# A 100-pair top-16 search, doubled lookup indices, and 44 row products beside the building of the gate table

## The chip, the core and the metric

The kernel runs on one core of one Trainium2 chip. The metric is the device time of one execution in microseconds (us). A run of a kernel is judged by the median of its executions.

## The reference, cut to what matters

The program is one step of a two-layer network for 384 tokens: 128 prompt tokens and 256 sample tokens. Each layer mixes the tokens by attention and then passes them through a retrieval of experts, which is where the change lies:

```
s1 = einsum('thd,nd->thn', q[..., :half], sub_k1)      # 8 heads, 128 keys
s2 = einsum('thd,nd->thn', q[..., half:], sub_k2)
v1, i1 = top_k(s1, 16);  v2, i2 = top_k(s2, 16)
cand_s = v1[..., :, None] + v2[..., None, :]           # 16 x 16 pairs per token and head
cand_i = i1[..., :, None] * 128 + i2[..., None, :]
top_s, pos = top_k(cand_s, 16)
idx = take_along_axis(cand_i, pos);  g = softmax(top_s)
out = sum over the 8 x 16 picks:  g * gelu(u_tab[idx] . x) * v_tab[idx]
```

The tables u and v have 16384 rows of 1024 numbers. Each token picks 8 x 16 = 128 of them.

## The kernel before, in words

The five engines have programs of their own, written out by hand, and meet at semaphores. No scheduler moves anything: the order in the code is the order on each engine. Both layers have the same experts part, about 900 us in each layer.

**Two ways through the tables.** For the 256 sample tokens the kernel computes against *all* rows: the tables are streamed in as 128 blocks of 128 experts, each block one 512 KB u chunk and one 512 KB v chunk. `hidden(b)` multiplies a u chunk with the tokens, ScalarE applies gelu, VectorE multiplies with the block's part of a gate table G (zero where an expert was not picked), which is `product(b)`, and `outer(b)` multiplies the result with the v chunk. For the 128 prompt tokens the kernel fetches just the picked rows: for each of 128 picks GpSimd issues one indirect DMA, which brings one u row for every token (128 x 1024 numbers, 512 KB). `dot(k)` on VectorE makes the row product. Later 128 more such DMAs bring the v rows, and `accumulate(k)` adds them up.

**Stages of the experts part of a layer.**

1. *Hidden stage.* TensorE does `hidden(0)` to `hidden(PLAIN - 1)`, `PLAIN` = 36, while VectorE searches: `top16` (five VectorE instructions per list: MAX8, FIND_INDEX8, MATCH_REPLACE8, MAX8, FIND_INDEX8) over lists of 128 key scores, then `winners`, which adds the 16 x 16 pairs and takes the 16 best of 256, then `pairs`, which turns places into key numbers by comparing with an iota, multiplying with the key numbers and reducing. ScalarE takes the exponents of the scores after gelu 12 (prompt) and gelu 29 (sample). `picks` then turns the results round on TensorE.
2. *Table stage.* TensorE does the `hidden` blocks that are left up to 63, and between them the 32 pieces of G (8 tokens each, `build(p)`); `pieces_of` spreads the pieces evenly over the blocks from `PLAIN` to `BUILT` = 62. For each piece VectorE makes four one-hot tensors (`one_hots(p)`), and after some of them an early `dot`. The early rows have only two places in memory (slots 4 and 5), as the four others lie where the one-hots are: the gather of row r + 2 waits for dot r.
3. *Middle stage.* TensorE does the 64 outer products of blocks 0 to 63; their gelu results come back from DRAM. VectorE does a product and about one dot for each (`MIDDLE_DOTS` = 72 in all). Rows have six slots from here on.
4. *Late stage.* For blocks 64 to 127 TensorE alternates `hidden(b + 1)`, now in three exact parts with u split into a high half (ScalarE) and a low half (VectorE, `low_u`), and `outer(b)`. VectorE does for each block a product, a `low_u`, and three rows: first the dots that are left (128 - 15 - 72 = 41), then from block 80 on the 128 sums, spread over 44 blocks.

**Queues.** SyncE loads all chunks in order into a ring of four slots, each load waiting until the slot is used up. In the late stage the loads go v, u, v, u. GpSimd issues the gathers in order. VectorE works strictly in order: when a `dot` waits for its row, the one-hots or products behind it wait too, and with them TensorE.

The lines that the prediction speaks of: 966 `hidden` in stages 1 and 2, 945 `build`, 931 `picks`, 977 `outer`, 670 to 672 `hidden` in the late stage, 1733 to 1745 `top16`, 1787 to 1793 `pairs`, 1834 to 1839 the one-hots, 1848 `product`, 1859 `low_u`, 1868 `dot`, 1882 `accumulate`, 1236 the high half of u, 589 the gathers.

Of the kernel before, what the change touches and what calls it, by code (L numbers as in the profile page):

```python
# [22 lines left out]
U32 = mybir.dt.uint32  # L23
# [17 lines left out]
HEADS = 8  # L41
TOPK = 16
KEYS = 128
STOK = TOK - P
# [3 lines left out]
SPILL = 64  # L48
PLAIN = 36
BUILT = 62  # L50
ROWS = 6
FULL = 4
EARLY_DOTS = 15
MIDDLE_DOTS = 72
GLS = 4
# [66 lines left out]
Q_IT = Q_IOE + KEYS // 2  # L122
Q_SW = Q_IT + 2 * STOK
Q_RING = Q_G - ROWS * D
# [43 lines left out]
def build(nc, a):  # L168
    ctx = ExitStack()
    with ctx:  # L170
# [129 lines left out]
        IOT = ar(Q_IOT, OA_N).bitcast(F16).rearrange("p (e t) -> p e t", e=KEYS)  # L300
        IT16 = ar(Q_IT, 2 * STOK).bitcast(F16).rearrange("p (q t) -> p q t", q=4)
        MROW = ar(A_MROW, 1024).rearrange("p (i n) -> p i n", i=2)
# [749 lines left out]
        def _(act):  # L1052
# [128 lines left out]
            def experts(l):  # L1181
# [29 lines left out]
                for b in range(SPILL):  # L1211
                    gelu(b)
                    if b == 12:
                        exponents(0, 0, P)
                    if b == 29:
                        exponents(1, P, STOK)
                    if b == PLAIN - 1:
                        for q in range(3):
                            act.wait_ge(sem("pick_ps"), since("pick_ps", l) + q + 1)
                            fn(IT16[:, q, :] if q < 2 else SW, ps[:, 3 + q, 0:STOK], ACT.Copy,  # L1220
                               scale=1.0 if q < 2 else G_SCALE).then_inc(sem("it_ready"), 1)
                    if b >= PLAIN:
                        for p in pieces_of(b):
                            part(p)
# [17 lines left out]
                for b in range(SPILL, KEYS):  # L1242
                    if b == SPILL:
                        gelu(b)
                    if b + 2 < KEYS:
                        high_u(b + 2)
                    if b + 1 < KEYS:
                        gelu(b + 1)
                    if b == SPILL + 15:
# [133 lines left out]
        def _(dve):  # L1383
# [337 lines left out]
            def retrieve(l):  # L1721
# [3 lines left out]
                dve.tensor_copy(IOT, iota.unsqueeze(2).to_broadcast([P, KEYS, PIECE]))  # L1725
                dve.tensor_copy(IOE, iota)

                IF16 = ar(Q_IF, NT * 128).bitcast(F16)
# [23 lines left out]
                dve.tensor_copy(IF16, ar(Q_I, NT * 256).bitcast(U32))  # L1752

# [4 lines left out]
                Tf = ar(Q_TV, NT * 128).rearrange("p (m n) -> p m n", n=TOPK)  # L1758
                IFh = IF16.rearrange("p (t h j n) -> p t h j n", t=NT, h=HEADS, j=2)
                eq = ar(Q_EQ, 1024).bitcast(F16)  # L1760

                def winners(first, last):

                    for t in range(first, last):
                        ins = tt(ar(Q_S + 2048 * t, 2048).rearrange("p (h a b) -> p h a b", h=HEADS, a=TOPK),
                                 Vh[:, t, :, 0, :].unsqueeze(3).to_broadcast([P, HEADS, TOPK, TOPK]),
                                 Vh[:, t, :, 1, :].unsqueeze(2).to_broadcast([P, HEADS, TOPK, TOPK]), ALU.add)
                    link(ins)
                    top16([(C[:, t, h, :], TV[:, t, h, :], TP[:, t, h, :])
                           for t in range(first, last) for h in range(HEADS)])  # L1770
                    m = slice(HEADS * first, HEADS * last)
                    link(dve.tensor_copy(ss[:, m], Tf[:, m, 0]))
                    tt(Tf[:, m], Tf[:, m], ss[:, m].unsqueeze(2).to_broadcast([P, HEADS * (last - first), TOPK]),
                       ALU.subtract).then_inc(sem("tv_ready"), 1)

                def pairs(first, last):

                    r, n = P * first, P * (last - first)
                    pos = ar(Q_TP + r, n).bitcast(U32)
                    ts(ar(Q_AB + r, n).bitcast(U32), pos, 4, None, ALU.logical_shift_right)  # L1780
                    link(ts(ar(Q_AB + 384 + r, n).bitcast(U32), pos, 15, None, ALU.bitwise_and))
                    for j in range(2):
                        ins = dve.tensor_copy(ar(Q_ABF + 384 * j + r, n), ar(Q_AB + 384 * j + r, n).bitcast(U32))
                    link(ins)
                    for j in range(2):
                        for t in range(first, last):
                            link(tt(eq.rearrange("p (m n) -> p m n", n=TOPK),
                                    ar(Q_ABF + 384 * j + 128 * t, 128).unsqueeze(2).to_broadcast([P, 128, TOPK]),
                                    iota[:, 0:TOPK].unsqueeze(1).to_broadcast([P, 128, TOPK]), ALU.is_equal))
                            e4 = eq.rearrange("p (h k n) -> p h k n", h=HEADS, k=TOPK)  # L1790
                            link(tt(e4, e4, IFh[:, t, :, j, :].unsqueeze(2).to_broadcast([P, HEADS, TOPK, TOPK]),
                                    ALU.mult))
                            link(dve.tensor_reduce(ar(Q_ID + 128 * (NT * j + t), 128),
# [24 lines left out]
            def experts(l):  # L1818
                at = {name: since(name, l) for name in ("gelu", "w_ready", "g_ps", "e1_ready", "row_used")}

                dve.wait_ge(sem("it_ready"), since("it_ready", l) + 3)
                link(dve.tensor_copy(IT16[:, 2, :], SW))
                link(tt(IT16[:, 3, :], SW, IT16[:, 2, :], ALU.subtract))

                def one_hots(p):
# [12 lines left out]
                    tt(high, low, over(2), ALU.mult)  # L1838
                    tt(low, low, over(3), ALU.mult).then_inc(sem("oh_ready"), 1)

# [64 lines left out]
                for b in range(SPILL, KEYS):  # L1905
# [12 lines left out]
                    if b == SPILL + 16:  # L1918
# [130 lines left out]
```

## Time and profile before

| | |
|---|---|
| median of 3 executions | 2618.59 us (2615.31 to 2625.87) |
| the profiled execution | 2623.26 us, its span 2621.4 us |
| TensorE (PE) busy | 2436.7 us, 93% of the span |
| VectorE (DVE) busy | 1707.4 us, 65% |
| GpSimd (POOL) busy | 914.4 us, 35% |
| ScalarE (ACT) busy | 639.3 us, 24% |
| moved by DMA | 679.61 MB |

Busy shares are means over stages with different limits, so they say little here. The windows view gives the same per stage, the timeline lists single instructions with the idle time ahead of them, and the chain of waits is followed back from the last instruction.

### The profile page before, as it was taken

The page shows a single profiled execution, that of the slowest core. Times are in us where ns is not written, and L with a number is a line of the kernel's source. Part 1 is how long each engine was busy: PE and PEld are TensorE (multiplying, and loading weights), DVE is VectorE, ACT ScalarE, POOL GpSimd, SP SyncE. Part 2 cuts the span into 40 slices and gives each one's busy share as a digit, 9 for nine tenths or more (in the row PEclk, how much of TensorE's full clock was granted, in tenths as well). Part 3 has the DMA queues.
Part 4 walks back from the last instruction along what each step waited for, and adds up shares of the span by engine and source line. Part 5 has one row for each costly group of instructions (what it writes and reads, how often), then busy time and mean ns, then how long its engine had stood idle before and what let it go on. Part 6 is the DMA issues. An engine that isn't in the chain of part 4 may idle for free.

```text
span 2621.4 us, 32722 instructions
## 1 busy us (share of the span) xinstructions
PE 2436.7 (93%) x12294; PEld 1755.8 (67%) x12294; DVE 1707.4 (65%) x3380; ACT 639.3 (24%) x1190; POOL 914.4 (35%) x650
## 2 busy tenths in 40 slices
PE   5988889999999999999978778999999999999995
PEld 4756689889544566666656567988974446666663
DVE  1345479979544676777645446897965457678775
ACT  2354441123000122222243344212320002221221
POOL 3400360001333454566353214200123335456550
PEclk8999989999999999999989798999999999999997
DMA  6455334656899999999835612265679999999992
GB/s 261 138 178 192 131 112 128 206 184 210 326 353 363 349 402 354 384 397 399 309 114 154 190 35 87 98 207 180 208 262 366 366 359 369 356 380 384 398 389 93
DMA packets 219899, 679.61 MB, mean 259 GB/s; under 512 B 32384, under 2 KB 63152, under 8 KB 219232
## 3 DMA queue, kind: packets, MB, share of 16 engines
q1 hardware_dynamic: 142912, 396.42, 43.2%
q0 software_dynamic: 76832, 281.11, 28.4%
q8 instruction: 99, 1.62, 0.2%
q14 instruction: 56, 0.46, 0.1%
HBM read 658.87 MB, written 18.56 MB: 258 GB/s over the span
## 4 chain that ended last, share of the span: by engine, by line
PE 73%; DMA 10%; DVE 8%; issue 4%; ACT 4%; SPq 1%; POOL 1%; ACTq 0%; DVEq 0%
PE ps L977 26%; PE ps L966 17%; DMA ring<-in_u 8%; PE ps L670 6%; PE ps L671 6%; PE ps L672 6%; DVE arena L1882 3%; PE ps L945 2%; PE ps L852 2%; PE ps L833 2%; ACT u_split L1236 1%; PE ps L693 1%; PE ps L842 1%; PE ps L701 1%; PE ps L920 1%
## 5 line engine op out<-in xcount | busy, mean ns | idle before, releaser
L977 PE MATMUL ps<-ring,arena 128*128 128x512 f32 x2048 | 903.8, 594 | 25.4 <-DVE arena L1848 24.7
L977 PEld LDWEIGHTS ps<-ring,arena 128*128 128x128 f32 x2048 | 379.7, 190 | 464.9 <-issue 464.7
L589 POOL DMA_INDIRECT arena<-in_u_rows,arena x256 | 300.1, 1172 | 856.1 <-DVE arena L1868 663.8
L966 PE MATMUL ps<-arena,ring 128*128 128x256 f32 x2048 | 454.1, 380 | 0.0
L589 POOL DMA_INDIRECT arena<-in_v,arena x256 | 355.7, 1389 | 252.9 <-DVE arena L1882 170.8
L966 PEld LDWEIGHTS ps<-arena,ring 128*128 128x128 f32 x2048 | 385.1, 190 | 50.0
L549 POOL TENSOR_TENSOR ring_lo<-ring,ring_hi 128x1024 fp32r<-128x1024 f32 x84 | 216.5, 2588 | 435.8 <-ACT ring_hi L1077 435.7
L1882 DVE SCALAR_TENSOR_TENSOR arena<-arena 128x1024 f32<-128x1024 f32 x254 | 325.8, 1282 | 19.4 <-DMA arena<-in_v,arena 1.9
L670 PE MATMUL ps<-xs_split,u_split 128*128 128x256 f32 x1024 | 336.2, 328 | 0.7 <-DVE u_split L1859 0.6
L1868 DVE CUSTOM_DVE_ANT_0 arena<-arena 128x1024 f32<-128x1024 f32 x256 | 307.1, 1220 | 8.5 <-DMA arena<-in_u_rows,arena 8.5
L1236 ACT ACTIVATE u_split<-ring 128x1024 fp32r<-128x1024 f32 x128 | 135.5, 1058 | 700.5 <-DMA ring<-in_u 660.5
L671 PE MATMUL ps<-xs_split,u_split 128*128 128x256 f32 x1024 | 289.3, 282 | 0.0
L672 PE MATMUL ps<-xs_split,u_split 128*128 128x256 f32 x1024 | 289.2, 282 | 0.0
L1859 DVE TENSOR_TENSOR u_split<-ring,u_split 128x1024 fp32r<-128x1024 f32 x128 | 156.8, 1225 | 180.2 <-ACT u_split L1236 164.3
L1848 DVE SCALAR_TENSOR_TENSOR arena<-arena 128x256 f32<-128x256 f32 x256 | 108.0, 423 | 243.6 <-DMA arena<-gelu_half 214.5
L670 PEld LDWEIGHTS ps<-xs_split,u_split 128*128 128x128 f32 x1024 | 195.4, 191 | 36.2 <-issue 36.2
L671 PEld LDWEIGHTS ps<-xs_split,u_split 128*128 128x128 f32 x1024 | 195.8, 191 | 27.3 <-issue 27.0
L1195 ACT ACTIVATE arena<-ps 128x256 f32<-128x256 f32 x256 | 97.3, 380 | 436.6 <-PE ps L966 338.4
L672 PEld LDWEIGHTS ps<-xs_split,u_split 128*128 128x128 f32 x1024 | 195.5, 191 | 0.0
L670 PE MATMUL ps<-ring_hi,x_hi 128*128 128x512 f32 (+2 forms) x312 | 122.2, 392 | 10.6 <-POOL x_lo L567 8.4
L671 PE MATMUL ps<-ring_lo,x_hi 128*128 128x512 f32 (+2 forms) x312 | 120.4, 386 | 0.0
L672 PE MATMUL ps<-ring_hi,x_lo 128*128 128x512 f32 (+2 forms) x312 | 120.1, 385 | 0.0
(223 smaller groups left out, 2736.8 us busy)
## 6 DMA issues: line engine op xcount, KB each, us to landing
ring<-in_u SPq DMA_DIRECT2D x256, 512.0 KB
ring<-in_v SPq DMA_DIRECT2D x256, 512.0 KB
ring<-in_w_mod SPq DMA_DIRECT2D x80, 512.0 KB
ring<-in_w_in SPq DMA_DIRECT2D x36, 512.0 KB
ring<-in_w_q SPq DMA_DIRECT2D x32, 512.0 KB
gelu_half<-arena SPq DMA_DIRECT2D x120, 128.0 KB, 3.5
arena<-gelu_half SPq DMA_DIRECT2D x120, 128.0 KB
arena<-in_w_mod SPq DMA_DIRECT2D x16, 512.0 KB, 18.9
```

Source lines behind the costliest of these rows:

```text
L549: pool.tensor_tensor(slot_lo[pos], slot[pos], f32(slot_hi[pos]), ALU.subtract).then_inc(lo_done(pos), 1)
L589: pool.indirect_dma_start(row[at], None, table, bass.IndirectOffsetOnAxis(where[:, k:k + 1], axis=0)).then_inc(sem(f"row_in{at}"), 16)
L670: mm(out, x[0], y[0], start=first, stop=False, skip_group_check=check)
L671: mm(out, x[0], y[1], start=False, stop=False, skip_group_check=check)
L672: return mm(out, x[1], y[0], start=False, stop=last, skip_group_check=check)
L966: ins = mm(ps[:, 6 + b % 2, 0:STOK], slot[c % RING][:, P * k:P * k + P], HFS[:, k, :], start=(k == 0), stop=(k == KC - 1))
L977: ins = mm(ps[:, t + 3 * q, :], GL[:, b % GLS, P * t - P:P * t], slot[c % RING][:, 512 * q:512 * q + 512], start=(b == MIDDLE[0]), stop=(b ...
L1236: fn(u_half(b, 0), slot[u_chunk(l, b) % RING], ACT.Copy).then_inc(sem("us_hi"), 1)
L1848: stt(w, w, 1.0 / G_SCALE, G[:, b, :], ALU.mult, ALU.mult).then_inc(sem("w_ready"), 1)
L1859: tt(u_half(b, 1), slot[c % RING], f32(u_half(b, 0)), ALU.subtract).then_inc(used(c % RING), 1)
L1868: dve.tensor_tensor_reduce(row[row_slot[k]], row[row_slot[k]], HP, 1.0, 0.0, ALU.mult, ALU.add, HSEL[:, k:k + 1]).then_inc(sem("row_used"), 1)
L1882: stt(HP, x, WSEL[:, k:k + 1], HP, ALU.mult, ALU.add).then_inc(sem("row_used"), 1)
```

## The change

Three things are changed together, and five constants with them.

*The search.* Of the 256 pairs of two sorted lists only those can be among the best 16 whose places i and j (from 0) meet (i + 1)(j + 1) <= 16. The new lists hold the first three i with all 16 j, and the other 13 i with the first four j: 3 x 16 + 13 x 4 = 100 pairs. The place in the list no longer is 16 i + j, so `pairs` finds the first key by comparing the place with the 16 starts of the rows and adding up differences of key numbers, and the second by a few more small instructions.

*The doubled indices.* Numbers that were read once and spread over the last dimension are now stored twice side by side, in 16 bits, and spread so that the last dimension is a run of two: in the comparisons of `pairs` (32 bits before) and in the second one-hot of a piece (16 bits before).

*The row products.* `EARLY_DOTS` goes from 15 to 44 and may be two after one piece, `MIDDLE_DOTS` from 72 to 60, so that 24 dots (41 before) are left for the late stage. `PLAIN` goes from 36 to 27, so the table stage has 35 blocks in place of 26 for the same 32 pieces. The sums start at block 76 and are spread over 48 blocks. The exponents are taken after gelu 10 and 20.

```diff
+WIDE, THIN = 3, 4
+CANDS = WIDE * TOPK + (TOPK - WIDE) * THIN
-PLAIN = 36
+PLAIN = 27
-EARLY_DOTS = 15
-MIDDLE_DOTS = 72
+EARLY_DOTS = 44
+MIDDLE_DOTS = 60
+SUMS = SPILL + 4 + (KEYS - EARLY_DOTS - MIDDLE_DOTS) // 3
...
-                    if b == 12:
+                    if b == 10:
                         exponents(0, 0, P)
-                    if b == 29:
+                    if b == 20:
                         exponents(1, P, STOK)
...
+                            if q == 1:
+                                fn(PAIRED, ps[:, 4, 0:STOK].unsqueeze(2).to_broadcast([P, STOK, 2]), ACT.Copy
+                                   ).then_inc(sem("it_ready"), 1)
...
-                        ins = tt(ar(Q_S + 2048 * t, 2048).rearrange("p (h a b) -> p h a b", h=HEADS, a=TOPK),
-                                 Vh[:, t, :, 0, :].unsqueeze(3).to_broadcast([P, HEADS, TOPK, TOPK]),
-                                 Vh[:, t, :, 1, :].unsqueeze(2).to_broadcast([P, HEADS, TOPK, TOPK]), ALU.add)
+                        tt(wide, Vh[:, t, :, 0, 0:WIDE].unsqueeze(3).to_broadcast([P, HEADS, WIDE, TOPK]),
+                           Vh[:, t, :, 1, :].unsqueeze(2).to_broadcast([P, HEADS, WIDE, TOPK]), ALU.add)
+                        ins = tt(thin, Vh[:, t, :, 0, WIDE:].unsqueeze(3).to_broadcast([P, HEADS, TOPK - WIDE, THIN]),
+                                 Vh[:, t, :, 1, 0:THIN].unsqueeze(2).to_broadcast([P, HEADS, TOPK - WIDE, THIN]), ALU.add)
...
-                    top16([(C[:, t, h, :], TV[:, t, h, :], TP[:, t, h, :])
+                    top16([(C[:, t, h, 0:CANDS], TV[:, t, h, :], TP[:, t, h, :])
...
-                            link(tt(eq.rearrange("p (m n) -> p m n", n=TOPK),
-                                    ar(Q_ABF + 384 * j + 128 * t, 128).unsqueeze(2).to_broadcast([P, 128, TOPK]),
-                                    iota[:, 0:TOPK].unsqueeze(1).to_broadcast([P, 128, TOPK]), ALU.is_equal))
+                            link(tt(eq.rearrange("p (m n i) -> p m n i", n=TOPK // 2, i=2),
+                                    (column if j else place)[:, P * t:P * t + P].unsqueeze(2).to_broadcast([P, 128, TOPK // 2, 2]),
+                                    (IOE[:, 0:TOPK] if j else STARTS).rearrange("p (n i) -> p n i", i=2).unsqueeze(1)
+                                    .to_broadcast([P, 128, TOPK // 2, 2]), ALU.is_equal if j else ALU.is_ge))
...
-                    tt(OB[:, p % 2], IT16[:, 1, col].unsqueeze(2).to_broadcast([P, PIECE, KEYS]),
-                       IOE.unsqueeze(1).to_broadcast([P, PIECE, KEYS]), ALU.is_equal)
+                    tt(OB[:, p % 2].rearrange("p t (e i) -> p t e i", i=2),
+                       PAIRED[:, col].unsqueeze(2).to_broadcast([P, PIECE, KEYS // 2, 2]),
+                       IOE.rearrange("p (e i) -> p e i", i=2).unsqueeze(1).to_broadcast([P, PIECE, KEYS // 2, 2]),
+                       ALU.is_equal)
...
-                    if dots < EARLY_DOTS * p // (PIECES - 1):
+                    while dots < EARLY_DOTS * p // (PIECES - 1):
                         dot(dots)
                         dots += 1
...
-                    while b >= SPILL + 16 and sums < P and 44 * sums < P * (b - SPILL - 15):
+                    while b >= SUMS and sums < P and (KEYS - SUMS - 4) * sums < P * (b - SUMS + 1):
                         accumulate(sums)
```

On TensorE, where the hidden stage of a layer ends and the table stage begins (`ps<-const,arena` is `picks`, 8 rows `ps<-arena,ring` are one block, 16 rows `ps<-arena` one piece), before:

```order
L920 MATMUL ps<-arena 128x128 x6
L966 MATMUL ps<-arena,ring 128x256 x288
L931 MATMUL ps<-const,arena 128x128 x6
L966 MATMUL ps<-arena,ring 128x256 x8
L945 MATMUL ps<-arena 128x128 x16
```

The same place in the changed kernel:

```order
L925 MATMUL ps<-arena 128x128 x6
L971 MATMUL ps<-arena,ring 128x256 x216
L936 MATMUL ps<-const,arena 128x128 x6
L971 MATMUL ps<-arena,ring 128x256 x16
L950 MATMUL ps<-arena 128x128 x16
```

`picks` moves from behind 36 blocks to behind 27, and there are now two blocks between it and the first piece where there was one.

On VectorE, in the middle of the table stage (L1834 to L1839 are the one-hots of a piece, the two L1868 rows are one dot and the read of its sum), before:

```order
L1839 TENSOR_TENSOR arena<-arena 128x1024
L1868 ISA arena<-arena 128x1024
L1868 ISA arena 128x1
L1834 TENSOR_TENSOR arena<-arena 128x1024
L1835 TENSOR_TENSOR arena<-arena 128x1024
L1838 TENSOR_TENSOR arena<-arena 128x1024
L1839 TENSOR_TENSOR arena<-arena 128x1024
L1834 TENSOR_TENSOR arena<-arena 128x1024
```

The same engine and stage in the changed kernel (L1863 to L1870 the one-hots, L1899 the dots):

```order
L1863 TENSOR_TENSOR arena<-arena 128x1024
L1864 TENSOR_TENSOR arena<-arena 128x1024
L1869 TENSOR_TENSOR arena<-arena 128x1024
L1870 TENSOR_TENSOR arena<-arena 128x1024
L1899 ISA arena<-arena 128x1024
L1899 ISA arena 128x1
L1899 ISA arena<-arena 128x1024
L1899 ISA arena 128x1
L1863 TENSOR_TENSOR arena<-arena 128x1024
```

A dot stood behind every second piece; now one or two stand behind each.

On VectorE, where the sums of the late stage begin (L1848 a product, L1859 a `low_u`, L1874 the weights, L1884 and L1882 the sums), before:

```order
L1874 TENSOR_TENSOR arena<-arena 128x128
L1884 TENSOR_SCALAR arena<-arena 128x1024
L1882 SCALAR_TENSOR_TENSOR arena<-arena 128x1024 x2
L1848 SCALAR_TENSOR_TENSOR arena<-arena 128x256
L1859 TENSOR_TENSOR u_split<-ring,u_split 128x1024
L1882 SCALAR_TENSOR_TENSOR arena<-arena 128x1024 x3
```

The same in the changed kernel (L1879, L1890, L1905, L1915 and L1913 in that order of roles):

```order
L1905 TENSOR_TENSOR arena<-arena 128x128
L1879 SCALAR_TENSOR_TENSOR arena<-arena 128x256
L1890 TENSOR_TENSOR u_split<-ring,u_split 128x1024
L1915 TENSOR_SCALAR arena<-arena 128x1024
L1913 SCALAR_TENSOR_TENSOR arena<-arena 128x1024 x2
L1879 SCALAR_TENSOR_TENSOR arena<-arena 128x256
L1890 TENSOR_TENSOR u_split<-ring,u_split 128x1024
L1913 SCALAR_TENSOR_TENSOR arena<-arena 128x1024 x3
L1879 SCALAR_TENSOR_TENSOR arena<-arena 128x256
L1890 TENSOR_TENSOR u_split<-ring,u_split 128x1024
L1913 SCALAR_TENSOR_TENSOR arena<-arena 128x1024 x2
```

The sums start four blocks earlier, the weights are made one block ahead of them, and blocks with two sums now stand among those with three.

## Rows read from the trace of the kernel before

**Rows 1.** The page: shares of the chain that ended last, by engine.

```profile
PE 73%; DMA 10%; DVE 8%; issue 4%; ACT 4%; SPq 1%; POOL 1%; ACTq 0%; DVEq 0%
```

**Rows 2.** Timeline of PE: start, us, instruction, count, idle time before.

```profile
417.28 124.49 PE L966 MATMUL ps<-arena,ring 128*128 128x256 f32 x576
...
546.92 1.21 PE L945 MATMUL ps<-arena 128*128 128x128 f16 x16 [1.04 <-DVE arena L1839]
```

**Rows 3.** Windows: stretch, length, busy time per engine, granted clock, DMA share, GB/s.

```profile
541.60:673.10 131.50, 130.46 (x966) 117.42 (x965) 115.66 (x165) 45.79 (x95) 18.48 (x18) 1.00 0.62 197
673.10:893.40 220.30, 219.72 (x513) 97.19 (x513) 108.46 (x202) 3.97 (x4) 78.88 (x72) 1.00 0.98 362
...
1019.40:1281.00 261.60, 252.33 (x1269) 174.31 (x1268) 207.53 (x196) 54.21 (x79) 161.63 (x117) 1.00 1.01 392
...
2293.40:2554.10 260.70, 250.11 (x1249) 172.00 (x1249) 205.20 (x194) 53.35 (x78) 158.34 (x116) 1.00 1.00 387
```

**Rows 4.** The chain in order of time, late stages: start, us, what.

```profile
899.80 3.44 PE ps L977 x8
906.11 3.45 PE ps L977 x8
909.95 9.61 DMA ring<-in_u
...
921.95 3.44 DVE arena L1868 x6
...
1288.20 3.44 PE ps L977 x8
...
2168.70 3.44 PE ps L977 x8
...
2561.06 3.67 PE ps L977 x8
```

**Rows 5.** Waits of 893.4 to 1281 us: engine, line, whom for; us, times, longest.

```profile
ACT u_split L1236 <- DMA ring<-in_u: 268.0, 59, 7.0
```

**Rows 6.** Timeline of DVE, end of the search and first pieces.

```profile
527.37 0.43 DVE L1802 TENSOR_TENSOR arena<-arena,ss 128x256 f32<-128x256 f32 x1
543.05 0.29 DVE L1822 CAST arena<-arena 128x256 f16<-128x256 f32 x1 [15.26 <-ACT arena L1220]
...
543.84 0.69 DVE L1834 TENSOR_TENSOR arena<-arena 128x1024 f16<-128x1024 f16 x1
544.44 1.22 DVE L1835 TENSOR_TENSOR arena<-arena 128x1024 f16<-128x1024 f16 x1
...
546.78 0.68 DVE L1834 TENSOR_TENSOR arena<-arena 128x1024 f16<-128x1024 f16 x1
```

**Rows 7.** DVE's groups in 417.3 to 545 us by shape: busy, mean ns.

```profile
L1787 DVE TENSOR_TENSOR arena<-arena,const 128x2048 f16<-128x2048 f32 x6 | 13.8, 2292 | 0.2
...
L1736 DVE FIND_INDEX8 arena<-arena 128x8 uint32<-128x256 f32 x24 | 9.5, 421 | 0.0
...
L1791 DVE TENSOR_TENSOR arena<-arena 128x2048 f16<-128x2048 f16 x6 | 7.3, 1225 | 0.2
...
L1736 DVE FIND_INDEX8 arena<-arena 128x8 uint32<-128x128 f32 x12 | 3.2, 284 | 0.0
```

**Rows 8.** Timeline of DVE, dots: the last column is the wait for the row.

```profile
564.61 1.22 DVE L1868 CUSTOM_DVE_ANT_0 arena<-arena 128x1024 f32<-128x1024 f32 x1
...
671.25 1.23 DVE L1868 CUSTOM_DVE_ANT_0 arena<-arena 128x1024 f32<-128x1024 f32 x1 [2.73 <-DMA arena<-in_u_rows,arena]
...
675.72 1.23 DVE L1868 CUSTOM_DVE_ANT_0 arena<-arena 128x1024 f32<-128x1024 f32 x1 [0.52 <-DMA arena<-in_u_rows,arena]
```

**Rows 9.** Timeline of POOL, gathers: when they are issued.

```profile
566.10 0.94 POOL L589 DMA_INDIRECT arena<-in_u_rows,arena  x1 [8.06 <-DVE arena L1868]
...
666.82 0.94 POOL L589 DMA_INDIRECT arena<-in_u_rows,arena  x1 [14.62 <-PE ps L945]
...
669.30 0.94 POOL L589 DMA_INDIRECT arena<-in_u_rows,arena  x1 [0.30 <-issue]
```

More of the change, by code:

```diff
@@ L122 @@
 Q_IT = Q_IOE + KEYS // 2
-Q_SW = Q_IT + 2 * STOK
+Q_SW = Q_IT + 5 * STOK // 2
 Q_RING = Q_G - ROWS * D
@@ L300, in build @@
         IOT = ar(Q_IOT, OA_N).bitcast(F16).rearrange("p (e t) -> p e t", e=KEYS)
-        IT16 = ar(Q_IT, 2 * STOK).bitcast(F16).rearrange("p (q t) -> p q t", q=4)
+        IT16 = ar(Q_IT, 5 * STOK // 2).bitcast(F16).rearrange("p (q t) -> p q t", q=5)
+        PAIRED = ar(Q_IT + STOK // 2, STOK).bitcast(F16).rearrange("p (t i) -> p t i", i=2)
+        STARTS = ar(Q_IT, TOPK // 2).bitcast(F16)
         MROW = ar(A_MROW, 1024).rearrange("p (i n) -> p i n", i=2)
@@ L1726, in retrieve @@
                 dve.tensor_copy(IOE, iota)
+                ts(ar(Q_IT + P, TOPK), iota[:, 0:TOPK], 4.0, 36.0, ALU.mult, ALU.add)
+                link(ts(ar(Q_IT + 2 * P, TOPK), iota[:, 0:TOPK], 16.0, None, ALU.mult))
+                tt(STARTS, ar(Q_IT + P, TOPK), ar(Q_IT + 2 * P, TOPK), ALU.min)
                 IF16 = ar(Q_IF, NT * 128).bitcast(F16)
@@ L1759, in retrieve @@
                 IFh = IF16.rearrange("p (t h j n) -> p t h j n", t=NT, h=HEADS, j=2)
+                STEPS = ar(Q_IF + NT * 128, NT * 64).bitcast(F16).rearrange("p (t h n) -> p t h n", t=NT, h=HEADS)
+                tt(STEPS[:, :, :, 1:].rearrange("p t h n -> p (t h) n"), IFh[:, :, :, 0, 1:].rearrange("p t h n -> p (t h) n"),
+                   IFh[:, :, :, 0, 0:TOPK - 1].rearrange("p t h n -> p (t h) n"), ALU.subtract)
+                link(dve.tensor_copy(STEPS[:, :, :, 0:1].rearrange("p t h n -> p (t h) n"),
+                                     IFh[:, :, :, 0, 0:1].rearrange("p t h n -> p (t h) n")))
                 eq = ar(Q_EQ, 1024).bitcast(F16)
@@ L1779, in pairs @@
                     pos = ar(Q_TP + r, n).bitcast(U32)
[L1780 to L1784, printed above, removed]
+                    low, mid = ar(Q_AB + r, n), ar(Q_AB + 384 + r, n)
@@ new lines, in pairs @@
+                    lowf, midf = ar(Q_EQ + 1024, n), ar(Q_EQ + 1024 + STOK, n)
+                    ts(low.bitcast(U32), pos, TOPK - 1, None, ALU.bitwise_and)
+                    link(ts(mid.bitcast(U32), pos, TOPK - THIN, None, ALU.bitwise_and))
+                    dve.tensor_copy(lowf, low.bitcast(U32))
+                    link(dve.tensor_copy(midf, mid.bitcast(U32)))
+                    place, column = (ar(Q_ABF + 384 * j, 384).bitcast(F16).rearrange("p (n i) -> p n i", i=2)
+                                     for j in range(2))
@@ L1785, in pairs @@
+                    dve.tensor_copy(mid, pos)
+                    link(dve.tensor_copy(place[:, r:r + n], pos.unsqueeze(2).to_broadcast([P, n, 2])))
+                    link(stt(midf, mid, float(WIDE * TOPK), midf, ALU.is_ge, ALU.mult))
+                    link(tt(column[:, r:r + n], lowf.unsqueeze(2).to_broadcast([P, n, 2]),
+                            midf.unsqueeze(2).to_broadcast([P, n, 2]), ALU.subtract))
                     for j in range(2):
                         for t in range(first, last):
-                            link(tt(eq.rearrange("p (m n) -> p m n", n=TOPK),
-                                    ar(Q_ABF + 384 * j + 128 * t, 128).unsqueeze(2).to_broadcast([P, 128, TOPK]),
-                                    iota[:, 0:TOPK].unsqueeze(1).to_broadcast([P, 128, TOPK]), ALU.is_equal))
+                            link(tt(eq.rearrange("p (m n i) -> p m n i", n=TOPK // 2, i=2),
+                                    (column if j else place)[:, P * t:P * t + P].unsqueeze(2).to_broadcast([P, 128, TOPK // 2, 2]),
+                                    (IOE[:, 0:TOPK] if j else STARTS).rearrange("p (n i) -> p n i", i=2).unsqueeze(1)
+                                    .to_broadcast([P, 128, TOPK // 2, 2]), ALU.is_equal if j else ALU.is_ge))
@@ L1834, in one_hots @@
                     tt(low, over(0), IOT[:, :, :], ALU.is_equal).then_inc(sem("e1_ready"), 1)
-                    tt(OB[:, p % 2], IT16[:, 1, col].unsqueeze(2).to_broadcast([P, PIECE, KEYS]),
-                       IOE.unsqueeze(1).to_broadcast([P, PIECE, KEYS]), ALU.is_equal)
+                    tt(OB[:, p % 2].rearrange("p t (e i) -> p t e i", i=2),
+                       PAIRED[:, col].unsqueeze(2).to_broadcast([P, PIECE, KEYS // 2, 2]),
+                       IOE.rearrange("p (e i) -> p e i", i=2).unsqueeze(1).to_broadcast([P, PIECE, KEYS // 2, 2]),
+                       ALU.is_equal)
                     dve.wait_ge(sem("e1_ready"), at["e1_ready"] + p + 1)
-                    tt(high, low, over(2), ALU.mult)
-                    tt(low, low, over(3), ALU.mult).then_inc(sem("oh_ready"), 1)
+                    tt(high, low, over(3), ALU.mult)
+                    tt(low, low, over(4), ALU.mult).then_inc(sem("oh_ready"), 1)
                 def product(b):
```

21 lines of the change are left out of this document (12 added, 9 removed).

## The prediction

> **What bounds the kernel now.** I read the chain of waits first. TensorE holds 73% of it and DMA 10% [rows 1]: the time is the matmuls plus what TensorE waits for, and no edit here takes a matmul away. So I looked, by the windows and then by the timeline, for the places where TensorE waits in the experts part, since only those can give something back.
>
> The hidden stage has none: 36 blocks take 124.49 us without a gap, 3.45 us each [rows 2]. The table stage has one, 1.04 us, where the first piece waits for its one-hots [rows 2]; after that 130.46 of 131.5 us are busy [rows 3]. The late stage has many. Its outer products start 6.31 us apart when nothing is late (899.80 to 906.11) [rows 4], and 59 such steps lead from block 64 to block 123, 372.3 us. They took 388.4 us in layer 0 (899.80 to 1288.20) and 392.4 us in layer 1 (2168.70 to 2561.06) [rows 4]: 16.1 and 20.1 us are lost. The chain says to what: from 909.95 a load of u holds it for 9.61 us, and what stands behind the load on VectorE, three dots of together 3.44 us, comes next [rows 4]. ScalarE waits for u in 59 of these 64 blocks, 268 us in all [rows 5]. Those loads are slow because the queues are full: while the sums run, the DMA share is 1.01 and 1.00, at 392 and 387 GB/s; in the table stage it is 0.62, at 197 GB/s [rows 3]. The granted clock is 1.00 throughout [rows 3], so nothing is to be had from it.
>
> **The change part by part, for one layer.**
>
> *The search must be done sooner.* `picks` now comes behind 27 blocks, at 417.28 + 27 x 3.45 = 510.4 us, and the search ended at 527.8 (the last gate) [rows 2, 6]. What gets shorter: a FIND_INDEX8 takes 421 ns over 256 numbers and 284 over 128 [rows 7], 1.07 ns a number. Over 100 numbers it takes 156 x 1.07 = 167 ns less; I take the same for the other four instructions of a list, and 24 lists save 5 x 24 x 0.167 = 20.0 us. The adding of pairs goes from 2048 to 800 numbers for each of three groups of tokens: 1248 x 1.07 ns x 3 = 4.0 us, less three more instructions' start, some 0.15 each. The six comparisons go from 32 to 16 bits, 2292 to 1225 ns if they run as the multiplications do, 6.4 us [rows 7]. Added are two instructions for the differences and eight in place of four per call of `pairs`, on at most 512 numbers, some 3 us at the durations above. The search ends near 501 us, 9 us before it is needed; without the faster comparisons near 507, still in time. VectorE's idle 15.26 us [rows 6] shrink and TensorE sees nothing: 0. The exponents of the sample tokens are asked for nine blocks sooner, 31 us, and their scores come some 22 us sooner; if they had been just in time, gelu would wait 9 us, and I charge 0, as the search then still had its whole decoding ahead and 15 us to spare.
>
> *The table stage starts earlier but is no shorter.* The 64 blocks and 32 pieces are the same matmuls. Only the wait of 1.04 us goes, since two blocks now stand ahead of the first piece: -1.0.
>
> *The one-hots.* A piece takes 2.94 us on VectorE (543.84 to 546.78), of which the second one-hot has 1.14 where the first has 0.60 [rows 6]. In pairs I take 0.60, so a piece takes 2.40. The trace has no row of an operand read in runs of two: the bounds are those two rows, and I take the fast one, because the first one-hot already reads a short run (eight numbers) again and again at that rate. The Trainium skill's Vector Engine (DVE) Microarchitecture Reference, section 5.1 on performance modes, says that two results per cycle ask for 16-bit operands, a step of one and more than one element in the innermost dimension, and that one element read again ran at one per cycle; 1.22 against 0.69 us for the same 1024 numbers [rows 6] agrees with its second half, and no row shows the first. By it the piece takes 2.40 too.
>
> *The early dots.* A dot takes 1.22 us of which 1.15 count [rows 8]. VectorE's work in the stage is 32 x 2.40 + 44 x 1.15 = 127 us, TensorE's 37 x 3.45 + 32 x 1.04 = 161 us: by work VectorE has room. What has not is the pair of row slots. A slot comes back after the dot (1.22), GpSimd's start (564.61 + 1.22 to 566.10, 0.27) [rows 8, 9], and the time L from issue to row. Before, 15 dots in 131.5 us on two slots left each slot some 17 us to come back. L shows only where dots do wait: the first of a burst 4.43 us (666.82 to 671.25), the third 6.42 (669.30 to 675.72) [rows 8, 9]. Dots 0 to 41 must be done before the last one-hots, some 142 us for 20 returns of each slot, 7.1 each; with 1.5 around it L may be 5.6. The two rows' mean is 5.4, but in that burst seven more rows pressed behind them; with at most two under way I take 5.1. Half a microsecond of slack per return remains, while a row can land behind a piece of 2.40 that has just begun. I charge +2.0; the bounds are 0 at 4.43 and 20 x (7.94 - 7.1) = 17 at 6.42, some 20 with those delays.
>
> The Trainium skill's DMA: Bandwidth & Descriptors, section on the anatomy of one DMA, fits 2.0 us plus bytes over 436 GB/s, an estimate of 3.2 us for 512 KB. By that the +2.0 would be 0; the rows, at 4.43 and more, do not bear it out.
>
> *The late stage.* This is where the gain must come from. A block moves two chunks and, while sums run, 128/44 = 2.91 rows, 4.91 x 0.524 = 2.57 MB; at 6.31 us that is 408 GB/s, more than the 392 and 387 that the full queues moved [rows 3, 4]. At 390 GB/s a block takes 6.60 us, 0.29 x 44 = 13 us lost, most of the 16.1 and 20.1. With 128/48 = 2.67 rows it is 2.45 MB, 388 GB/s: just what was moved. Seventeen dots fewer (24, not 41) also shorten the first stretch with three rows per block from 14 blocks to 8. In steady state nothing is lost then, but without margin, and one late load still costs (three rows stand behind it). I leave 5 of 16.1 and 5 of 20.1: -11 and -15. Bounds: all of it (-16, -20), or a third (-5, -7) if the loss is in the order of waits more than in bytes.
>
> *Nothing elsewhere.* In the middle stage TensorE is busy for 219.72 of 220.3 us [rows 3], and 60 dots in place of 72 only take load away. Gelu, copies and the stores to DRAM stay.
>
> *Sum.* -11 - 15 for the late stages, 2 x (-1.0 + 2.0) for the table stages: -24. From the profiled 2623.3 us (span 2621.4 and 1.9 around it) that is 2599; that execution lay 4.7 above the median of 2618.6, so the median should become 2594 or 2595. I say 2594.
>
> **The rivals.**
>
> *All of the loss goes.* No row waits in the table stage and the late stage keeps its step: -36 - 2, 2580. For it: the demand falls to the queues' rate on average. Against it: no margin.
>
> *The loss stays.* If the late blocks are slowed by the chain load, high half, low half, three rows, product, and not by bytes, two thirds stay: -12 + 2, 2608 to 2612. For it: the load of 9.61 us and the dots behind it stand in one chain [rows 4]. Against it: a share of 1.01 [rows 3].
>
> *The slots turn into the bound (slower).* The table stage will move about 290 GB/s now (37 u chunks, 33 stores of 128 KB and 44 rows in 161 us), against 197 [rows 3], so L grows; at 6.42 the stage is 17 to 20 us longer per layer, VectorE stands in a dot, the one-hots behind it are late and TensorE waits at `build`. That is +40 - 28 = +12 or more: 2630 to 2635. It decides from L of about 6.2 on, where the loss (20 x 0.65 = 13) eats the gain. For it: 6.42 is in the trace. Against it: only in a burst of nine. 
>
> *The pairs are not fast.* The piece stays at 2.94 and VectorE has 32 x 2.94 + 44 x 1.15 = 145 us of work against the 142 that the last one-hots leave it: 3 over, and late rows of 2 to 4 no longer hidden, so 7 instead of 2 per layer, 2604.
>
> **Chances.** Forecast 0.45 (2586 to 2603), all gone 0.20, loss stays 0.17, pairs not fast 0.06, slots bound 0.12. A measurement of this kernel can tell about 0.5%, 13 us. Faster than 2605.5: 0.45 + 0.20 + most of 0.06, 0.70. Slower than 2631.7: 0.08 of the slots' 0.12. Within: 0.22. The range 2578 to 2616 leaves out the slots' case and a little below.
>
> **What would show it.** `picks` at about 510 us without idle time before it; second one-hot near 0.69 us; dots of the table stage waiting on rows some tens of us in all while TensorE's wait at `build` stays within 5 us; late steps of 6.31 us with about 5 us lost per layer, DMA share below 1.00 while the sums run. I am wrong if TensorE waits for one-hots over 10 us per layer, or if late steps stay at 6.6 us with fewer bytes.

## The result, and the profile after

The changed kernel is slower: 2638.15 us (median of 4, 2634.38 to 2646.71) against 2616.95 us for the kernel before on the same chip (median of 4), a ratio of 1.0086 with a 95% interval of 1.0066 to 1.0105, or 21 us more. The prediction was 2594 us, faster. In the profiled executions the difference is smaller, 2634.4 against 2623.3 us.

The chain that ended last now runs less through TensorE and more through DMA and VectorE than before [rows 1]:

```profile
PE 64%; DMA 15%; DVE 13%; ACT 4%; issue 3%; SPq 1%; POOL 1%; ACTq 0%; DVEq 0%
```

The search did what was forecast. The groups of VectorE by shape (busy, mean ns) during it show the shorter lists and the faster comparison, which took 2292 ns before [rows 7]:

```profile
L1815 DVE TENSOR_TENSOR arena<-arena 128x2048 f16<-128x2048 f16 x6 | 7.4, 1225 | 0.2
L1748 DVE FIND_INDEX8 arena<-arena 128x8 uint32<-128x100 f32 x24 | 5.6, 256 | 0.0
```

The hidden stage is 27 blocks without a gap (start, us, instruction, count), and VectorE, done with the last gate at 494.42, waits 10.26 us for what ScalarE brings back from `picks`. The one-hots that follow now all take the same time; the second had 1.22 us before [rows 6]:

```profile
409.79 93.41 PE L971 MATMUL ps<-arena,ring 128*128 128x256 f32 x432
```

```profile
494.00 0.42 DVE L1831 TENSOR_TENSOR arena<-arena,ss 128x256 f32<-128x256 f32 x1
504.69 0.29 DVE L1851 CAST arena<-arena 128x256 f16<-128x256 f32 x1 [10.26 <-ACT arena L1229]
...
505.48 0.69 DVE L1863 TENSOR_TENSOR arena<-arena 128x1024 f16<-128x1024 f16 x1
506.09 0.68 DVE L1864 TENSOR_TENSOR arena<-arena 128x1024 f16<-128x1024 f16 x1
```

The windows show where the time went: the table stages of both layers (from `picks` to the first middle outer product), the middle stage of layer 0, and the late stages from block 64's outer product to block 123's. The columns are the stretch, its length, each engine's busy time, the granted clock, the DMA share and GB/s, as in [rows 3]:

```profile
502.82:677.72 174.90, 164.27 (x1112) 144.05 (x1110) 132.95 (x222) 50.02 (x104) 50.26 (x47) 1.00 0.83 267
1780.65:1958.89 178.24, 164.85 (x1111) 143.79 (x1110) 132.90 (x223) 50.01 (x104) 50.49 (x46) 1.00 0.82 262
903.31:1288.19 384.88, 376.36 (x1891) 259.87 (x1889) 278.16 (x297) 82.21 (x121) 202.56 (x147) 1.00 0.95 363
2184.47:2572.13 387.66, 376.57 (x1891) 259.54 (x1889) 278.62 (x297) 82.83 (x120) 200.93 (x147) 1.00 0.95 360
```

```profile
677.72:897.23 219.51, 219.51 (x513) 97.28 (x512) 96.92 (x183) 4.12 (x4) 62.29 (x62) 1.00 0.95 340
```

The middle stage loses nothing. A table stage in which TensorE never waits takes 161.90 us (two experiments below show it), so 13.0 and 16.3 us are lost there, where before 1.04 was. The late stages take 12.6 and 15.4 us more than the 372.3 of 59 undisturbed steps, where before 16.1 and 20.1 were lost [rows 4]. That is +12 and +15 for the table stages and -3.5 and -4.7 for the late ones, +19 in all, near the 21 between the medians. In the profiled executions layer 0's hidden stage also began 7.5 us sooner (409.79 against 417.28 [rows 2]), so these two executions differ by only 11; I return to that at the end.

From 512 to 665 us, nearly all of layer 0's table stage, the chain has no piece of TensorE in it. Its shares between 500 and 680 us, and a stretch of it in order of time (start, us, what):

```profile
by line: DMA arena<-in_u_rows,arena 48.4%; DVE arena L1899 17.3%; PE ps L971 11.5%; DVE arena L1863 4.4%; DVE arena L1869 4.4%; DVE arena L1870 4.3%; DVE arena L1864 4.3%; issue 2.2%; PE ps L950 1.8%; PE ps L982 1.2%; PE ps L936 0.4%
```

```profile
583.40 1.16 DVE arena L1899 x2
584.82 6.94 DMA arena<-in_u_rows,arena
591.78 1.24 DVE arena L1899 x2
593.28 4.56 DMA arena<-in_u_rows,arena
597.87 1.25 DVE arena L1899 x2
599.37 7.37 DMA arena<-in_u_rows,arena
606.76 1.23 DVE arena L1899 x2
```

A dot, the gather into the slot that it frees, the next dot on that slot: the slots' round trip sets the pace. Outside this stretch the one-hots (L1863 to L1870, 17% together) stand in the chain too. VectorE works in order, so a late row also holds up the one-hots behind its dot, and behind those the dot that would free the *other* slot. The waits of 503 to 672 us agree (us in total, times, longest): the dots wait for rows, and TensorE at `build` waits for VectorE's last one-hot:

```profile
DVE arena L1899 <- DMA arena<-in_u_rows,arena: 35.7, 25, 2.5
...
PEld ps L950 <- DVE arena L1870: 15.2, 12, 2.1
PE ps L950 <- DVE arena L1870: 10.6, 10, 1.7
```

How long is a round trip? On GpSimd's timeline the gather behind dot 0 starts at 511.79 and the 42nd, behind dot 41, at 666.79. The gathers go to the two slots in turn, so the 41 steps between them, 155.0 us, are 20.5 round trips of each slot, 7.56 us each. In layer 1 the same two gathers start at 1789.62 and 1948.90: 159.3 us, 7.77 each. The view of DMA issues from 511 to 667 us (the last column is the median us from issue to landing, over the rows whose landing is on record) gives 5.4 for the landing alone.

```profile
511.79 0.94 POOL L594 DMA_INDIRECT arena<-in_u_rows,arena  x1 [58.34 <-DVE arena L1899]
```

```profile
666.79 1.15 POOL L594 DMA_INDIRECT arena<-in_u_rows,arena  x1 [2.41 <-DVE arena L1899]
```

```profile
arena<-in_u_rows,arena POOLq DMA_INDIRECT x42, 5.4
```

The late stage's chain is the one of before [rows 4], with sums in the place of dots:

```profile
1146.14 10.10 DMA ring<-in_u
...
1156.32 1.06 ACT u_split L1245
...
1158.55 1.29 DVE arena L1913
...
1159.94 1.29 DVE arena L1913
...
1161.68 1.28 DVE arena L1913
1162.96 0.34 DVE arena L1879
```

The load of u releases the high half on ScalarE (L1245), this releases the low half on VectorE (L1890), and behind the low half VectorE does three sums. Only then comes the product (L1879) of the block *before*, for which TensorE's outer product (L982) waits. VectorE's and TensorE's timelines show both waits, and the waits of 903 to 1288 us show how often TensorE has the second:

```profile
1157.41 1.23 DVE L1890 TENSOR_TENSOR u_split<-ring,u_split 128x1024 fp32r<-128x1024 f32 x1 [5.99 <-ACT u_split L1245]
```

```profile
1163.44 3.67 PE L982 MATMUL ps<-ring,arena 128*128 128x512 f32 x8 [1.55 <-DVE arena L1879]
```

```profile
PE ps L982 <- DVE arena L1879: 7.8, 13, 1.6
```

The product's own inputs were seldom late: in the same stretch VectorE waited for a gelu before a product twice, 2.5 us in all. It waited in VectorE's line, while VectorE stood idle for the low half.

### The profile page after: what moved, and what is told of

Its sections match the earlier page's. It is cut to its first block, busy times and chain, and to the rows that moved or that the text cites. A ratio compares the mean times of both kernels' runs of the same rounds, so it can differ in the third digit from the quotient of the medians.

```text
span 2632.5 us, 32754 instructions
## 1 busy us (share of the span) xinstructions
PE 2433.3 (92%) x12294; PEld 1750.3 (66%) x12294; DVE 1625.0 (62%) x3412; ACT 641.1 (24%) x1190; POOL 890.0 (34%) x650
## 4 chain that ended last, share of the span: by engine, by line
PE 64%; DMA 15%; DVE 13%; ACT 4%; issue 3%; SPq 1%; POOL 1%; ACTq 0%; DVEq 0%
PE ps L982 27%; PE ps L971 8%; DMA ring<-in_u 8%; PE ps L675 6%; PE ps L676 6%; PE ps L677 6%; DMA arena<-in_u_rows,arena 6%; DVE arena L1913 3%; DVE arena L1899 3%; PE ps L857 2%; PE ps L838 1%; ACT u_split L1245 1%; PE ps L847 1%; PE ps L925 1%; PE ps L706 1%
## 5 line engine op out<-in xcount | busy, mean ns | idle before, releaser
L982 PE MATMUL ps<-ring,arena 128*128 128x512 f32 x2048 | 903.0, 593 | 18.8 <-DVE arena L1879 18.5
L982 PEld LDWEIGHTS ps<-ring,arena 128*128 128x128 f32 x2048 | 379.9, 190 | 456.3 <-issue 456.2
L594 POOL DMA_INDIRECT arena<-in_u_rows,arena x256 | 277.2, 1083 | 826.9 <-DVE arena L1899 691.0
L1899 DVE CUSTOM_DVE_ANT_0 arena<-arena 128x1024 f32<-128x1024 f32 x256 | 310.1, 1220 | 78.9 <-DMA arena<-in_u_rows,arena 78.5
L1913 DVE SCALAR_TENSOR_TENSOR arena<-arena 128x1024 f32<-128x1024 f32 x254 | 325.6, 1282 | 17.4 <-DVE arena L1913 0.9
L1245 ACT ACTIVATE u_split<-ring 128x1024 fp32r<-128x1024 f32 x128 | 135.4, 1058 | 654.2 <-DMA ring<-in_u 617.7
L1890 DVE TENSOR_TENSOR u_split<-ring,u_split 128x1024 fp32r<-128x1024 f32 x128 | 156.6, 1223 | 207.8 <-ACT u_split L1245 207.6
L1879 DVE SCALAR_TENSOR_TENSOR arena<-arena 128x256 f32<-128x256 f32 x256 | 107.9, 422 | 275.8 <-DMA arena<-gelu_half 236.7
```

Of the source, the lines that this page charges most:

```text
L594: pool.indirect_dma_start(row[at], None, table, bass.IndirectOffsetOnAxis(where[:, k:k + 1], axis=0)).then_inc(sem(f"row_in{at}"), 16)
L982: ins = mm(ps[:, t + 3 * q, :], GL[:, b % GLS, P * t - P:P * t], slot[c % RING][:, 512 * q:512 * q + 512], start=(b == MIDDLE[0]), stop=(b ...
L1245: fn(u_half(b, 0), slot[u_chunk(l, b) % RING], ACT.Copy).then_inc(sem("us_hi"), 1)
L1879: stt(w, w, 1.0 / G_SCALE, G[:, b, :], ALU.mult, ALU.mult).then_inc(sem("w_ready"), 1)
L1890: tt(u_half(b, 1), slot[c % RING], f32(u_half(b, 0)), ALU.subtract).then_inc(used(c % RING), 1)
L1899: dve.tensor_tensor_reduce(row[row_slot[k]], row[row_slot[k]], HP, 1.0, 0.0, ALU.mult, ALU.add, HSEL[:, k:k + 1]).then_inc(sem("row_used"), 1)
```

## The experiments

Theories for the table stage: *slots* (the round trip above), against *work* (VectorE is simply full) and *stage order* (the earlier `picks` or the new code). For the late stage: *order* (the product stands behind sums that stand behind a late low half) against *bytes* (the queues cannot bring more, the prediction's view).

**1. Thirty early dots, one per piece.**

```diff
-EARLY_DOTS = 44
-MIDDLE_DOTS = 60
+EARLY_DOTS = 30
+MIDDLE_DOTS = 74
```

> The changed kernel with 30 early dots (one a piece) in place of 44 and 74 in the middle stage in place of 60; the late stage keeps its 24 dots. Theory 'slots' (the table stage waits for rows that return through two slots): picks to first middle outer product falls from 174.9 and 178.2 us to 162 to 163 in both layers, the dots' wait for rows there nearly goes, and the time is 2638 - 28 = 2610 us (2605 to 2616). Rival 'stage order' (the loss comes with the earlier picks, the paired one-hot or the new search): the stages stay at 174 to 178 and the time at 2634 to 2640. Rival 'work' (VectorE is simply full with 44 dots) expects the same as 'slots' here. The late stages, 12.8 and 15.6 us lost, stay as they are.

Measured: 2609.89 us (12 runs), as *slots* said, 0.997 of the kernel before (0.9957 to 0.9984; its median on this chip was 2618.34). Its two table stages:

```profile
504.67:666.57 161.90, 161.90 (x1111) 145.06 (x1110) 116.86 (x195) 50.01 (x104) 31.01 (x34) 1.00 0.74 245
1770.01:1931.91 161.90, 161.90 (x1112) 145.06 (x1110) 116.98 (x195) 50.01 (x104) 31.35 (x34) 1.00 0.74 243
```

TensorE is busy for every microsecond of both. *Stage order* falls. The late stages lose 13.4 and 13.6 us, much as they did (12.6 and 15.4).

**2. All 44 dots, without their round trips.** Dots 3 to 44 run on the row that already lies in the slot, each once the dot that used the slot last is done, and their results are multiplied by 0.

```diff
-                    gather(l, r)
+                    if not 2 <= r < EARLY_DOTS:
+                        gather(l, r)
...
-                    row_in(k)
+                    if 2 <= k < EARLY_DOTS:
+                        dve.wait_ge(sem("row_used"), at["row_used"] + k - 1)
+                    else:
+                        row_in(k)
```

> The changed kernel with all its 44 early dots on VectorE, but only the first two of these rows are gathered; dots 3 to 44 go over the row that lies in the slot already (their results are left out of the output). Theory 'slots': VectorE's work is the same, the wait for rows is gone, the table stages take 162 to 163 us and the time is 2610 us (2605 to 2616). Rival 'work': the stages stay at 174 to 178, the time at 2634 to 2640. In between if the traffic of 84 rows fewer speeds up something else; the late stages should not change.

Measured: 2613.41 us (12 runs), 0.998 (0.9967 to 0.9994). The table stages:

```profile
505.53:667.43 161.90, 161.90 (x1111) 145.06 (x1110) 132.38 (x223) 50.05 (x104) 5.09 (x5) 1.00 0.50 154
1774.46:1936.36 161.90, 161.90 (x1111) 145.06 (x1110) 132.47 (x223) 50.06 (x104) 5.09 (x5) 1.00 0.49 154
```

VectorE's busy time is that of the changed kernel, 132.4 against 132.95, and TensorE waits for nothing. *Work* falls, *slots* stands. This run also takes 42 rows of traffic out of each stage; that this traffic slows TensorE by another way than the rows' lateness is excluded by run 1 for 30 rows, and by run 6 below for 38. One miss: the late stages should have stayed, but lost 18.3 and 18.9 us in its profile (893.27 to 1283.83 and 2161.85 to 2553.06). The profiled execution was the slowest of the twelve, 2619.83 us; why its late stages lost more stays open.

**3. The rows ahead of the low half, all else as changed.** In each late block VectorE's order is product, rows, low half:

```diff
                     product(b)
-                    if b + 2 < KEYS:
-                        low_u(b + 2)
...
                         accumulate(sums)
                         sums += 1
+                    if b + 2 < KEYS:
+                        low_u(b + 2)
```

> The changed kernel with one thing moved: in each late block VectorE does the dots or sums first and the low half of u behind them, in place of the low half first; bytes, rows and slots are the same. Theory 'order' (the product of the next block stands on VectorE behind the sums, and these behind a low half that waits for its load): of 12.8 and 15.6 us lost between blocks 64 and 123 under 4 and 4 stay, and the time is 2638 - 20 = 2618 us (2612 to 2624). Theory 'bytes' (the loads come at the queues' rate): the loss stays within 2 us of what it was, 2634 to 2641. If late rows now hold up the low half and with it the next load, the loss grows, above 2641. The table stages stay at 175 and 178.

Measured: 2610.53 us (10 runs), 0.9968 (0.9952 to 0.9983). The late stages of the same stretch of blocks:

```profile
910.63:1284.84 374.21, 372.96 (x1891) 258.55 (x1890) 280.87 (x297) 82.45 (x120) 205.24 (x147) 1.00 0.96 373
2180.18:2554.65 374.47, 373.01 (x1890) 258.37 (x1889) 280.87 (x297) 82.37 (x120) 209.45 (x147) 1.00 0.96 373
```

1.9 and 2.2 us are lost in place of 12.6 and 15.4, with the same bytes, rows and slots, and 373 GB/s where 363 were moved. VectorE's timeline shows the new order (two sums, low half, product):

```profile
1157.01 2.67 DVE L1913 SCALAR_TENSOR_TENSOR arena<-arena 128x1024 f32<-128x1024 f32 x2
1159.60 1.22 DVE L1890 TENSOR_TENSOR u_split<-ring,u_split 128x1024 fp32r<-128x1024 f32 x1
1160.74 0.42 DVE L1879 SCALAR_TENSOR_TENSOR arena<-arena 128x256 f32<-128x256 f32 x1
```

ScalarE waits for u no less than in the changed kernel. The waits of that stretch, first of the changed kernel, then of this one:

```profile
ACT u_split L1245 <- DMA ring<-in_u: 230.9, 56, 7.3
```

```profile
ACT u_split L1245 <- DMA ring<-in_u: 252.0, 58, 8.0
```

So ScalarE stands waiting for the loads as long as ever, and TensorE no longer notices: there is no wait of L982 for L1879 in that stretch any more. *Order* stands. The median lies 1.5 us below the range that *order* gave. The late stages gave back 23.9 us in the profile where 20 were expected; the few us beyond that are not explained, and the table stages of this profile were not shorter (181.4 and 178.6 us).

**4. Both edits.**

> Both edits together, 30 early dots and the rows ahead of the low half. With 'slots' and 'order' both right the two gains add, as they lie in different stages: 2638 - 28 - 20 = 2590 us (2584 to 2597), faster than the kernel before by 1%. With 'slots' alone 2610, with 'order' alone 2618.

Measured: 2587.05 us (6 runs), 0.9884 (0.9866 to 0.9901). Alone the two edits took 28.3 and 27.6 us off the changed kernel's 2638.15, together 51.1: the gains add, but for some 5 us. Layer 0's table and late stages:

```profile
503.61:665.52 161.91, 161.91 (x1112) 145.07 (x1111) 117.10 (x195) 50.01 (x104) 31.33 (x33) 1.00 0.75 245
893.18:1267.09 373.91, 372.90 (x1890) 258.56 (x1889) 281.06 (x297) 82.40 (x120) 202.87 (x147) 1.00 0.97 375
```

**5. The kernel before, with the rows ahead of the low half** (the edit of run 3 and nothing of the change).

> The kernel before, with nothing of the change, and the late blocks' dots or sums ahead of the low half of u. Its late stage still moves 2.91 rows a block. Theory 'order': between blocks 64 and 123 under 4 us stay lost of 16.3 and 20.5, the rest is as it was, 2618 - 32 = 2586 us (2580 to 2594), the same as the changed kernel with 30 early dots and this order. Theory 'bytes' in the form of the prediction (390 GB/s is all that the queues give, so a block with 2.91 rows takes 6.60 us): 13 us a layer stay lost, 2618 - 11 = 2607 us (2602 to 2613), and the change's fewer late rows are worth some 20 us.

Measured: 2592.04 us (6 runs), 0.9903 (0.9885 to 0.9922; before 2616.01 on this chip). Its late stages:

```profile
898.93:1277.14 378.21, 374.66 (x1891) 257.73 (x1890) 299.39 (x330) 80.30 (x120) 228.24 (x164) 1.00 1.00 394
2156.25:2535.15 378.90, 374.31 (x1891) 257.92 (x1889) 300.44 (x330) 79.95 (x119) 233.96 (x164) 1.00 1.00 395
```

The time lies in the range that *order* gave. 5.9 and 6.6 us are lost, not under 4 and not 13: some 10 and 13.5 us of the loss before were order. About 4 a layer more are lost than in run 3; I put them down to the 2.91 rows a block, but the two kernels differ by the whole change. The 390 GB/s of the prediction were no ceiling. In a stretch with sums alone (1019 to 1270 us), where the kernel before moved 392 GB/s, this one moves 404, nearly the 408 that the prediction held to be too many:

```profile
1019.00:1270.00 251.00, 248.19 (x1256) 170.86 (x1255) 205.02 (x195) 52.39 (x78) 158.99 (x114) 1.00 1.02 404
```

**6. Thirty-eight early dots, 66 in the middle, rows first.**

```diff
-EARLY_DOTS = 44
-MIDDLE_DOTS = 60
+EARLY_DOTS = 38
+MIDDLE_DOTS = 66
```

> The changed kernel with 38 early dots and 66 in the middle, and the rows ahead of the low half. Theory 'slots' with the return time that the changed kernel showed (21 returns of a slot in 155.0 us, 7.38 each): 18 returns take 133 of about 142 us, so the table stages stay at 162 to 164, and the time at 2587 us (2582 to 2592), as with 30. If the time of a return spreads so widely that a mean says little, each stage loses 3 to 8 us: 2593 to 2603.

Measured: 2585.37 us (5 runs, 2580.75 to 2585.71), 0.9877 (0.9858 to 0.9896). The table stages:

```profile
508.29:671.63 163.34, 162.11 (x1112) 144.97 (x1110) 125.85 (x211) 50.03 (x104) 43.89 (x41) 1.00 0.84 269
1760.78:1922.68 161.90, 161.90 (x1112) 145.06 (x1110) 126.25 (x211) 50.03 (x104) 43.74 (x41) 1.00 0.84 271
```

1.4 us and nothing lost, at as many GB/s as with 44 dots (267 and 262). So it is not the rate of the bytes: the round trips decide. The expectation's 21 and 18 round trips are 20.5 and 17.5 when counted between the first gather and the last; 17.5 of 7.56 us are 132 and fit in the 142 us that the last one-hots leave, 20.5 are 155 and do not. This is the lowest median of the kernels that were run, though run 4's 0.9884 cannot be told from it.

**7. The two dots of a piece spread, 44 in all, rows first.** Where a piece has two dots, the first stands between the comparisons and the multiplications:

```diff
+                    if between is not None:
+                        dot(between)
                     dve.wait_ge(sem("e1_ready"), at["e1_ready"] + p + 1)
...
-                    one_hots(p)
+                    two = EARLY_DOTS * p // (PIECES - 1) - dots == 2
+                    one_hots(p, dots if two else None)
+                    dots += two
```

> The changed kernel with its 44 early dots, rows ahead of the low half, and where a piece has two dots the first of them between the comparisons and the multiplications of the piece, so that two gathers are not issued 1.4 us apart. Theory 'pairs of gathers' (the second of two rows issued together lands late, 6 to 8 us, and the dot waits for it): the return of a slot falls from 7.4 to about 6.9 us, the table stages to about 165 from 181 and 179, the time to 2611 - 28 = 2583 to 2590 us. Theory 'load of the queues' (a row takes 5.7 us on the mean in this stage however it is issued): the stages stay above 174, the time at 2606 to 2613.

Measured: 2615.69 us (12 runs), 1.0006 (0.9992 to 1.002). The table stages:

```profile
505.23:689.46 184.23, 167.94 (x1111) 146.02 (x1110) 133.54 (x223) 50.02 (x104) 53.03 (x47) 0.98 0.80 256
1777.58:1957.08 179.50, 167.85 (x1112) 146.26 (x1110) 133.46 (x223) 50.01 (x104) 52.76 (x47) 0.98 0.81 261
```

A miss for *pairs of gathers*. In the chain (555 to 605 us) the gathers still take 4.88 to 8.00 us one after another; two of them:

```profile
572.21 6.43 DMA arena<-in_u_rows,arena
...
587.13 8.00 DMA arena<-in_u_rows,arena
```

The theory had little to stand on: in layer 0's table stage no two of these gathers start 1.4 us apart. The closest are 2.49 us apart in the changed kernel (559.45 and 561.94) and 1.76 in run 3, as the second dot of a piece often waits for its row itself. Here the closest are still 2.35 apart (557.76 and 560.11), so the edit hardly drew them apart, and the run hardly tests the theory. What makes a row take 5 to 8 us there stays open. The load of the queues was the other theory, and this run's failure does not show it; with 30 early dots (run 4, 245 GB/s) the median from issue to landing between 517 and 640 us was 5.8, no shorter than the 5.5 of the changed kernel between the same times. The time is also a little above the 2606 to 2613 that the theory gave.

## Why the prediction was wrong, step by step

- *The search sooner, 0*: right. It ended 84.6 us after the hidden stage began (494.42 against 409.79; the forecast's 501 against 417.28 is 84), and TensorE saw nothing.
- *First piece's wait, -1.0*: right; where TensorE never waits, the stage's 161.90 us are 0.9 less than the 131.74 of before (`picks` at 541.60 to the first outer product at 673.34) and nine blocks of 3.45.
- *One-hots of 2.40 us*: right (505.48 and 506.09 stand 0.61 apart). The rival of slow pairs is out.
- *The early dots, +2.0 a layer*: **this step failed**. It cost 13.0 and 16.3 us. The mechanism stood in the working, but the limit and the length of a round trip were both mis-sized. The limit: dots 0 to 41 are 20.5 round trips, not 20, so 142 us leave 6.9 each and L, the time from issue to row, may be 5.4, not 5.6. The length: L was taken as 5.1, below the mean of the rows that the trace offered. The burst had three dots that waited, not two (the second took 5.57 us, 668.06 to 673.63), and their mean is 5.5. What came was a median of 5.4 for the landing and 6.1 from a gather to its dot (7.56 less the 1.49 from dot 0 to its gather); for the difference, by an estimate some half a microsecond, the row lies there while its dot stands in VectorE's line. So 155.0 us stood against 142, 13 over, and 159.3 in layer 1, 17 over. A term that goes from 0 to 17 us within 2 us of L was booked at 2. The Trainium skill's DMA: Bandwidth & Descriptors, section on the anatomy of one DMA, fits 2.0 us plus bytes over 436 GB/s for a DMA that GpSimd issues, an estimate of 3.2 us for a row; the 5.4 here does not agree with it, and the 0 that it gave for this term is far from what came.
- *The late stage, -11 and -15*: **this step failed too**; -3.5 and -4.7 came. It was priced by bytes: 388 GB/s needed, 387 and 392 moved, so little lost. But the changed kernel moved 363 and 360 GB/s in steps nearly as long as before. Runs 3 and 5 show that the loss was VectorE's order: one edit that moves no byte takes out 10.7 and 13.2 of 12.6 and 15.4 us in the changed kernel, and 10 and 13.5 of 16.1 and 20.1 in the one before. Fewer rows, with the rest of the change, are worth about 4 us a layer. The text had this chain under *the loss stays*, with 17%, and held the DMA share of 1.01 against it. A full queue and a late product were both there; the late product made most of the loss, and at most the 5.9 and 6.6 us that run 5 leaves can be the queue's.
- *The rivals*: *the slots turn into the bound* gave 2630 to 2635 and *the loss stays* the rest; both came true together, and the chances treated them as alternatives. The slots rival's sum (+40 - 28) comes near the time with two terms that are each too large: +27 and -8 were measured.
- *What would make it wrong*: both signs that the text named were seen, TensorE waiting over 10 us a layer for one-hots (weight loads 15.2 and matmuls 10.6 us at `build` in layer 0, partly at the same time) and steps of 6.52 and 6.57 us (384.88 and 387.66 over 59; 6.58 and 6.65 before) with fewer bytes.

Open: the profiles of the changed kernel and of runs 1 to 4 and 7 begin layer 0's hidden stage 5 to 7.5 us before the kernel before, run 6 two, and run 5, which has nothing of the change, at the same time (417.41). What runs up to there is no part of the experts, and the change does not touch it; with one profile of each kernel I cannot say whether it goes with the change, and I have not found its cause. A third slot for early rows was not tried; the memory behind the one-hots is taken.

## What to carry to other kernels

Where work takes turns on a few buffers, count the round trips that the stage has room for and keep the whole round trip, dots, starts and the wait in line included, below the quotient with a margin: 17.5 trips of 7.56 us in 142 cost at most 1.4 us, 20.5 cost 13 and more. Count from the first dot to the last, as half a trip was the margin here. When an engine works in order and one of its waits is long, look at what stands *behind* the waiting instruction but does not need it: moving two or three sums ahead of one low half was worth 1%, more than the whole change in its best size added on top (2592 to 2585 us). A queue that is full beside a stall is a correlate until an experiment moves one without the other.

## What was not expected of the hardware

A DMA share of 1.01 did not mean that no more could be moved. The kernel before moved 392 and 387 GB/s at 1.01 and 1.00 while the sums ran [rows 3]; run 5, with the same loads and rows, moved 404 at 1.02.

The prediction had no row for the other, and had to choose between two: a half-precision comparison whose operand is read as runs of two, each run repeated 64 times, takes 0.68 us for 1024 numbers, the same as one with runs of eight; read as single numbers it took 1.22 us [rows 6].
